# Gate and up of the feed-forward projections computed as a pair, matmul by matmul into two PSUM banks

## Chip, cores and metric

The kernel runs on one core of a Trainium2 chip. The metric is the device time of one execution in microseconds; lower is better.

## What is computed

Two transformer blocks, one after the other, on a sequence of 512 tokens with 1024 features, in float32. The first block has two layers (stick-breaking attention, dilated attention), the second one layer (a gated recurrence and a differential attention, with a modulation computed from a vector). Each of the three layers ends in a feed-forward part of inner width 2816:

```python
def _swiglu(h, w_gate, w_up, w_down):
    return (jax.nn.silu(h @ w_gate) * (h @ w_up)) @ w_down
# layers 1 and 2
h = h + _swiglu(_rmsnorm(h, norm_ffn[layer]), w_gate[layer], w_up[layer], w_down[layer])
# second block
u = rmsnorm(h, norm2_w[l]) * (1.0 + sc2) + sh2
ff = (jax.nn.silu(u @ w_ffn_gate[l]) * (u @ w_ffn_up[l])) @ w_ffn_down[l]
h = h + g2 * ff
```

The products h @ w_gate and h @ w_up, three times, are what the change touches.

## The kernel before, in words

Activations lie with features on partitions: h, xh and xl have 8 tiles of 128 x 512. Each float32 product is made of three matmuls in a faster float32 form: every operand is split into a high part (rounded) and a low part (the rest), and high x high, high x low and low x high are summed in PSUM. xh and xl are the two parts of the input.

**Units.** The weights come as units: one unit holds the 8 (in some cases 6) 128 x 128 tiles that make one output tile of 128 features. For gate and up ("gu0", "gu1", "gu2") the units alternate: gate, up, gate, up, 44 per stage, in a loop of 11 rounds of 4 (j = 0 to 3). Units have a running number over the whole kernel. A unit goes through four steps, on four queues:

- SP loads it into raw (`load_units`, L260), once the unit three before it has its low split (L253 and after).
- ACT splits off the high part: whi <- raw (`split_hi`, L281 to L290). It waits for the load, and for PE to be done with the unit three before it (`mm_done` at number - 2, L289).
- DVE subtracts: wlo <- raw - whi (`split_lo`, L301).
- PE computes the product (`product`, L303 to L318): it waits for the low split, then for each of 8 tiles issues three matmuls (L314, L315, L316) into one PSUM bank and signals `mm_done` on the last.

raw, whi and wlo have four slots each. ACT and DVE split two units ahead of the one that their loop stands at (`ahead`).

**A feed-forward projection** (`ffn_act` L607, `ffn_dve` L621, `ffn_pe` L647). Unit j writes bank j. PE waits, before unit j, until DVE has read the banks two pairs back (`f.up`, L651). After each second unit (j odd) DVE waits for `mm_done` of that unit, multiplies gate and up by rstd out of PSUM (L631, L632; in the third projection plain copies, L635 and L636), ACT applies Silu (L615), DVE multiplies (L639), ACT and DVE make the high and low parts acth and actl (L617, L641). ACT loads an activation table at some of the changes between Silu and Copy.

**What stands around it.** The stage before is a residual projection of four-unit rounds (`res_pe`, `res_act`, `res_dve`), moving tiles oh and ol, whose results become h and then xh (L373) and xl (L383). POOL sums the squares of h (L406). In the first two projections the sum over partitions is a matmul with ones (`total`, L411), placed by `ffn_pe` behind the first unit's product (`behind_first`). DVE and ACT go on from it in program order: `refine` and `root` (L424, ACT L416 and L418, DVE L427 to L432) make rstd, and only after these stand the first splits of the feed-forward loop, those of units 2 and 3. Units 0 and 1 are split in the stage before. In the third projection PE sums before the stage, and DVE and ACT then make xh and xl tile by tile (`modulate_dve` L731, L739 and `modulate_act` L745); PE follows with the first unit, waiting for each tile (`ready`).

The stage behind is the down projection ("down0" to "down2") with moving tiles acth and actl.

Of the kernel before, what the change touches and what calls it, by code (L numbers as in the profile page):

```python
# [6 lines left out]
P = 128  # L7
S = 512
D = 1024
KT = D // P  # L10
# [43 lines left out]
def wait(eng, signal, value):  # L54

    if isinstance(value, int) and value <= 0:
        return
    if isinstance(signal, Since):
        eng.wait_ge(signal.sem, value + signal.base)
    else:  # L60
        eng.wait_ge(signal, value)
# [31 lines left out]
def build(nc, a, out):  # L93
    ctx = ExitStack()
    with ctx:
# [3 lines left out]
        def place(name, shape, dtype, at=None):  # L99
            size = int(np.prod(shape[1:])) * {F32: 4, F32R: 4, BF16: 2, U8: 1}[dtype]  # L100
            size = -(-size // 32) * 32
            if at is None:
                at, top[0] = top[0], top[0] + size
            t = nc.alloc_sbuf_tensor_at(name, shape, dtype, offset=at)
            return t

        def sem(name):
            return ctx.enter_context(nc.semaphore(name))
# [6 lines left out]
        xh = place("xh", [P, KT, S], F32R)  # L115
        xl = place("xl", [P, KT, S], F32R)
        raw = place("raw", [P, 4, UNIT], F32)
        whi = place("whi", [P, 4, UNIT], F32R)
        wlo = place("wlo", [P, 4, UNIT], F32R)
# [107 lines left out]
        ps = ctx.enter_context(nc.psum_tensor("ps", [P, 8, S], F32))  # L227
# [5 lines left out]
        lo_done = sem("lo_done")  # L233
        mm_done = sem("mm_done")
        phases = []
        before, used = 0, [0] * 4
        for name, count, body, ring in (("qkv", 8, 3, 3), ("o_a", 2, 4, 4), ("gu0", 11, 4, 4), ("down0", 4, 6, 3),
# [4 lines left out]
            u = Units(a[name], count, body, ring, before, used, widths)  # L242
# [38 lines left out]
        def split_hi(act, u, pos):  # L281

            if pos is None:
                return
            t, j = pos
            s, n = u.slot(j), u.widths[j] * P
            act.wait_ge(landed[s], u.landings(t, j))

            wait(act, mm_done, u.number(t, j) - 2)  # L289
            act.activation(whi[:, s, 0:n], raw[:, s, 0:n], ACT.Copy).then_inc(hi_done, 1)  # L290

        def split_lo(eng, u, pos, in_turn=False):
# [11 lines left out]
        def product(pe, u, t, j, bank, hi, lo, k0=0, start=True, stop=True, ready=None):  # L304

            pe.wait_ge(lo_done, u.number(t, j) + 1)
            s, n = u.slot(j), u.widths[j]
            for k in range(n):
                w = slice(k * P, (k + 1) * P)
                if callable(ready):  # L310
                    ready(k0 + k)
                elif ready is not None:
                    wait(pe, ready, k0 + k + 1)
                pe.matmul(ps[:, bank], whi[:, s, w], hi[:, k0 + k], start=start and k == 0, stop=False)  # L314
                pe.matmul(ps[:, bank], whi[:, s, w], lo[:, k0 + k], start=False, stop=False)  # L315
                mm = pe.matmul(ps[:, bank], wlo[:, s, w], hi[:, k0 + k], start=False,  # L316
                               stop=stop and k == n - 1)
            mm.then_inc(mm_done, 1)  # L318

        def hold(eng, signal, value):  # L320


            wait(eng, signal, value)
            if not isinstance(value, int):
                eng.sem_inc(held[eng], 1)
# [82 lines left out]
        def total(pe, r, bank):  # L408

            wait(pe, r.added, KT + 1)  # L410
            pe.matmul(ps[:, bank], ones[:, :], sqsum[:, :], start=True, stop=True).then_inc(r.total.sem, 1)  # L411
# [123 lines left out]
        def res_act(act, u, r, gain):  # L535
            per = 1 if u.body == 4 else 3

            def body(t, end=False):
                for j in range(u.body):
                    split_hi(act, u, ahead(u, t, j, end))  # L540
                    if j % per == per - 1:
                        m = t * (u.body // per) + (j // per)
                        residual_hi(act, r, m, gain)
                        residual_sq(act, r, m, (j // per) % 2)
            body(0)
            if u.count > 2:
                with act.Fori(1, u.count - 1) as t:
                    body(t)
            body(u.count - 1, True)
            root(act, r)  # L550
# [26 lines left out]
        def res_pe(pe, u, r, hi, lo, ready, ada=None, sum_now=True):  # L577

            per = 1 if u.body == 4 else 3

            def body(t):
                for j in range(u.body):
                    m = t * (u.body // per) + (j // per)
                    if j % per == 0 and per == 1:
                        wait(pe, r.h_new, m - 3)
                    elif j % per == 0:
                        wait(pe, r.h_new, m - 1)
                    k0 = 8 * (j % per)
                    first = isinstance(t, int) and t == 0 and j < per
                    product(pe, u, t, j, j // per, hi, lo, k0, start=j % per == 0, stop=j % per == per - 1,  # L590
                            ready=ready if first else None)
                    if ada is not None:

                        if j:
                            ada_tile(pe, ada, t, j - 1)
                        elif not isinstance(t, int):
                            ada_tile(pe, ada, t - 1, 5)
            body(0)
            if u.count > 1:
                with pe.Fori(1, u.count) as t:  # L600
                    body(t)
            if ada is not None:
                ada_tile(pe, ada, u.count - 1, 5)
            if sum_now:
                total(pe, r, 7)

        def ffn_act(act, u, f):  # L607
            def body(t):
                for j in range(4):
                    split_hi(act, u, ahead(u, t, j, False))  # L610
                    if j % 2:
                        i = j // 2
                        n = 2 * t + (i + 1)
                        wait(act, f.gate, n)
                        act.activation(tmp[i][:, :], tmp[i][:, :], ACT.Silu).then_inc(f.silu.sem, 1)  # L615
                        hold(act, f.prod, n)
                        act.activation(acth[:, 2 * t + i], tmp[2 + i][:, :], ACT.Copy).then_inc(f.hi.sem, 1)  # L617
            with act.Fori(0, u.count) as t:
                body(t)
# [27 lines left out]
        def ffn_pe(pe, u, f, ready, behind_first=None):  # L647

            def body(t):
                for j in range(4):  # L650
                    wait(pe, f.up, 2 * t + (j // 2 - 1))  # L651
                    first = isinstance(t, int) and j == 0
                    product(pe, u, t, j, j, xh, xl, ready=ready if first else None)
                    if first and behind_first is not None:
                        total(pe, behind_first, 7)
            body(0)
            with pe.Fori(1, u.count) as t:
                body(t)
# [398 lines left out]
        def _(act):  # L1057
            act.wait_ge(const_in, 32)
            act.wait_ge(filled, 1)
            setup_act(act)  # L1060
            split_hi(act, U["qkv"], (0, 0))
            split_hi(act, U["qkv"], (0, 1))
            for m in range(KT):
# [456 lines left out]
        def _(pe):  # L1520
# [11 lines left out]
            def stage_g(t):  # L1532
                for j in range(3):
                    if j == 0:
                        wait(pe, qkv_out, 3 * t)
                    elif j == 1:
                        if isinstance(t, int) and t == 0:
                            wait(pe, rin.rstd, 1)
                        wait(pe, v_tok, t)
                    else:  # L1540
                        pe.wait_ge(qkv_out, 3 * t + 1)
                    first = leading(t) and j == 0
                    product(pe, u, t, j, 6 + j % 2, xh, xl, ready=rin.x_lo if first else None)
                    if first:
                        total(pe, rin, 7)
# [302 lines left out]
```

## Time and profile before

| | |
|---|---|
| three runs | 2268.95, 2269.93, 2271.29 us; median 2269.93 |
| profiled execution, span from first to last instruction | 2266.9 us |
| PE (matmul) busy | 2076.2 us, 92% |
| PEld (weight loads) busy | 1622.6 us, 72% |
| DVE, ACT, POOL busy | 1192.0, 842.0, 328.7 us |
| mean granted TensorE clock | 0.943 |
| projections gate/up: first matmul of each | 377.16, 1060.33, 1875.30 us |

No other time is recorded for the profiled execution than its span; the median of the runs is 3.0 us above it. The profile's busy time of PE overstates the work, since matmuls are pipelined and each row lasts longer than its step: the cadence has to be read from starts. PEld is the loading of weights, which runs beside the matmul before. A clock of 1.00 is 2.4 GHz, 0.50 is 1.2 GHz.

### The profile page before, as it was taken

The numbers are of one execution on the slowest core, as the hardware profiler recorded it, in microseconds if no ns is written. First come the engines' busy times: TensorE is split into PE (matmuls) and PEld (weight loads), VectorE is DVE, ScalarE is ACT, GpSimd is POOL, SyncE is SP. The second block draws the span as 40 slices with busy tenths as digits, with TensorE's granted clock in tenths as the row PEclk, the third lists the DMA queues.
The fourth block names the chain that finished last, engine by engine and source line by source line (L and its number), as shares of the span: only waits on it lengthen the run. The fifth ranks groups of instructions, "written<-read, shape, count | busy, mean of one in ns | idle before, by whom it ended". The sixth has DMA issues, their size and how long they took to land.

```text
span 2266.9 us, 25387 instructions
## 1 busy us (share of the span) xinstructions
PE 2076.2 (92%) x9000; PEld 1622.6 (72%) x9000; DVE 1192.0 (53%) x1566; ACT 842.0 (37%) x1098; POOL 328.7 (15%) x285
## 2 busy tenths in 40 slices
PE   6999989999999799989999999487759788999997
PEld 4767667888888577757888888375546566888885
DVE  4423235444488645435444488777875545444323
ACT  4443434434422233334444322343333324443321
POOL 2000001000011144431000011354421110000000
PEclk9999889999999799999999999699969799999998
DMA  3101102332355211102332355121002022223331
GB/s 118 56 32 52 37 28 84 99 104 93 90 191 193 88 56 56 56 30 86 97 102 97 96 186 200 57 72 50 28 30 73 28 75 74 93 93 104 93 93 53
DMA packets 53108, 189.38 MB, mean 84 GB/s; under 512 B 5936, under 2 KB 6448, under 8 KB 52928
## 3 DMA queue, kind: packets, MB, share of 16 engines
q1 hardware_dynamic: 45504, 160.85, 21.6%
q0 software_dynamic: 7552, 27.86, 3.7%
q8 instruction: 30, 0.49, 0.1%
q14 instruction: 22, 0.18, 0.0%
HBM read 186.59 MB, written 2.10 MB: 83 GB/s over the span
## 4 chain that ended last, share of the span: by engine, by line
PE 77%; DVE 10%; issue 6%; ACT 3%; POOL 2%; DMA 0%; SPq 0%; DVEq 0%; ACTq 0%; POOLq 0%
PE ps L314 21%; PE ps L315 21%; PE ps L316 21%; PE ps L1556 2%; PE ps L759 2%; PE ps L794 2%; PE ps L1590 1%; PE ps L1574 1%; PE ps L777 1%; DVE wlo L301 1%; PE ps L1579 1%; DVE tmps L670 1%; POOL qlev L1034 1%; POOL sqsum L406 1%; DVE amat L1439 1%
## 5 line engine op out<-in xcount | busy, mean ns | idle before, releaser
L314 PE MATMUL ps<-xh,whi 128*128 128x512 f32 x1536 | 611.3, 398 | 28.5 <-DVE xl L739 16.4
L315 PE MATMUL ps<-xl,whi 128*128 128x512 f32 x1536 | 604.9, 394 | 0.0
L316 PE MATMUL ps<-xh,wlo 128*128 128x512 f32 x1536 | 604.5, 394 | 0.0
L301 DVE TENSOR_TENSOR wlo<-raw,whi 128x1024 fp32r<-128x1024 f32 (+1 forms) x292 | 367.2, 1267 | 233.8 <-ACT whi L290 229.6
L290 ACT ACTIVATE whi<-raw 128x1024 fp32r<-128x1024 f32 (+1 forms) x304 | 313.9, 1038 | 286.4 <-PE ps L316 277.9
L314 PEld LDWEIGHTS ps<-xh,whi 128*128 128x128 f32 x1536 | 293.4, 191 | 103.5 <-issue 25.4
L316 PEld LDWEIGHTS ps<-xh,wlo 128*128 128x128 f32 x1536 | 292.6, 191 | 61.8
L315 PEld LDWEIGHTS ps<-xl,whi 128*128 128x128 f32 x1536 | 293.4, 191 | 60.3 <-issue 0.5
L314 PE MATMUL ps<-acth,whi 128*128 128x512 f32 x528 | 212.1, 402 | 0.2
L406 POOL TENSOR_TENSOR sqsum<-sqsum,tmps 128x512 f32<-128x512 f32 x64 | 86.1, 1346 | 856.8 <-ACT tmps L376 850.6
L316 PE MATMUL ps<-acth,wlo 128*128 128x512 f32 x528 | 208.6, 395 | 0.0
L315 PE MATMUL ps<-actl,whi 128*128 128x512 f32 x528 | 208.3, 395 | 0.0
L615 ACT ACTIVATE tmps<-tmps 128x512 f32<-128x512 f32 x66 | 41.7, 632 | 292.5 <-DVE tmps L631 193.0
L316 PEld LDWEIGHTS ps<-acth,wlo 128*128 128x128 f32 x528 | 99.2, 188 | 23.6
L314 PEld LDWEIGHTS ps<-acth,whi 128*128 128x128 f32 x528 | 99.4, 188 | 22.0 <-issue 0.3
L315 PEld LDWEIGHTS ps<-actl,whi 128*128 128x128 f32 x528 | 99.4, 188 | 21.7
L631 DVE TENSOR_TENSOR tmps<-ps,rstd 128x512 f32<-128x512 f32 x44 | 30.4, 692 | 133.2 <-PE ps L316 133.2
L391 POOL DMA_DIRECT2D wada<-in_ada x24 | 13.2, 552 | 573.3 <-DVE actl L641 483.4
L873 POOL TENSOR_SCALAR prob<-prob,small 128x512 f32<-128x512 f32 (+1 forms) x64 | 74.5, 1182 | 68.4 <-DVE small L855 68.4
L376 ACT ACTIVATE tmps<-h 128x512 f32<-128x512 f32 (+1 forms) x56 | 34.9, 623 | 121.2 <-DVE h L567 72.8
L641 DVE TENSOR_TENSOR actl<-tmps,acth 128x512 f32 (+1 forms) x66 | 45.7, 693 | 64.9 <-ACT acth L617 64.9
L314 PE MATMUL ps<-oh,whi 128*128 128x512 f32 x192 | 77.1, 402 | 1.1 <-DVE ol L928 1.1
(234 smaller groups left out, 2686.8 us busy)
## 6 DMA issues: line engine op xcount, KB each, us to landing
raw<-in_gu SPq DMA_DIRECT2D x132, 512.0 KB, 3.4
raw<-in_down SPq DMA_DIRECT2D x48, 512.0 KB, 3.8
raw<-in_qkv SPq DMA_DIRECT2D x24, 512.0 KB, 3.4
wada<-in_ada POOLq DMA_DIRECT2D x24, 512.0 KB, 3.6
tmps<-in_ada POOLq DMA_DIRECT2D x24, 512.0 KB, 3.8
raw<-in_qkvb SPq DMA_DIRECT2D x24, 512.0 KB, 3.3
raw<-in_down SPq DMA_DIRECT2D x24, 384.0 KB, 3.1
raw<-in_recur SPq DMA_DIRECT2D x16, 512.0 KB, 3.4
```

Source lines behind the costliest of these rows:

```text
L290: act.activation(whi[:, s, 0:n], raw[:, s, 0:n], ACT.Copy).then_inc(hi_done, 1)
L301: eng.tensor_tensor(wlo[:, s, 0:n], raw[:, s, 0:n], whi[:, s, 0:n].bitcast(F32), ALU.subtract).then_inc(lo_done, 1)
L314: pe.matmul(ps[:, bank], whi[:, s, w], hi[:, k0 + k], start=start and k == 0, stop=False)
L315: pe.matmul(ps[:, bank], whi[:, s, w], lo[:, k0 + k], start=False, stop=False)
L316: mm = pe.matmul(ps[:, bank], wlo[:, s, w], hi[:, k0 + k], start=False, stop=stop and k == n - 1)
L406: pool.tensor_tensor(sqsum[:, :], sqsum[:, :], sq[m % 2][:, :], ALU.add).then_inc(r.added.sem, 1)
L615: act.activation(tmp[i][:, :], tmp[i][:, :], ACT.Silu).then_inc(f.silu.sem, 1)
L641: dve.tensor_tensor(actl[:, 2 * t + i], tmp[2 + i][:, :], acth[:, 2 * t + i].bitcast(F32), ALU.subtract).then_inc(f.lo.sem, 1)
L759: mm = pe.matmul(tri_ps[i][:, OFF[b]:OFF[b] + w], q[rows, c * P:(c + 1) * P], k[rows, 0:w], start=True, stop=True, skip_group_check=True)
L794: mm = pe.matmul(o, v, prt[i][:, OFF[b]:OFF[b] + S - b * P], start=b == 0, stop=b == NB - 1)
L873: pool.tensor_scalar(pr[i][:, w], pr[i][:, w], share[:, 4 * i + b:4 * i + b + 1], None, ALU.mult)\
L1556: pe.matmul(tri_ps[i][:, OFF[b]:OFF[b] + n], kT[rows, b * P:(b + 1) * P], qT[rows, b * P:S], start=b != 3, stop=False, skip_group_check=True)
```

## The change

A new routine takes two units at once. For each of the 8 tiles it issues six matmuls: high weights x high input for gate, then for up; high weights x low input for both; low weights x high input for both. The two go to banks j and j + 1 in turn. It waits at its start for the low split of both units. ACT's wait ahead of a high split asks, for the gate/up units, for the unit four before instead of three before. `ffn_pe` calls the routine for j = 0 and 2; the sum of squares (`total`) stands behind the first call.

```diff
-            wait(act, mm_done, u.number(t, j) - 2)
+            wait(act, mm_done, u.number(t, j) - (3 if u.name.startswith("gu") else 2))
             act.activation(whi[:, s, 0:n], raw[:, s, 0:n], ACT.Copy).then_inc(hi_done, 1)
...
+        def product_pair(pe, u, t, j, bank, hi, lo, ready=None):
+
+            pe.wait_ge(lo_done, u.number(t, j) + 2)
+            for k in range(KT):
+                w = slice(k * P, (k + 1) * P)
+                if ready is not None:
+                    wait(pe, ready, k + 1)
+                for weight, moving, step in ((whi, hi, 0), (whi, lo, 1), (wlo, hi, 2)):
+                    for n in range(2):
+                        mm = pe.matmul(ps[:, bank + n], weight[:, u.slot(j + n), w], moving[:, k],
+                                       start=k == 0 and step == 0, stop=k == KT - 1 and step == 2)
+                        if k == KT - 1 and step == 2:
+                            mm.then_inc(mm_done, 1)
...
             def body(t):
-                for j in range(4):
+                for j in (0, 2):
                     wait(pe, f.up, 2 * t + (j // 2 - 1))
                     first = isinstance(t, int) and j == 0
-                    product(pe, u, t, j, j, xh, xl, ready=ready if first else None)
+                    product_pair(pe, u, t, j, j, xh, xl, ready=ready if first else None)
                     if first and behind_first is not None:
                         total(pe, behind_first, 7)
```

## Rows read from the trace of the kernel before

**Rows 1.** The page: busy times, and the chain's shares by engine.

```profile
PE 2076.2 (92%) x9000; PEld 1622.6 (72%) x9000; DVE 1192.0 (53%) x1566; ACT 842.0 (37%) x1098; POOL 328.7 (15%) x285
...
PE 77%; DVE 10%; issue 6%; ACT 3%; POOL 2%; DMA 0%; SPq 0%; DVEq 0%; ACTq 0%; POOLq 0%
```

**Rows 2.** The page's costliest group: busy us, mean ns, idle before it.

```profile
L314 PE MATMUL ps<-xh,whi 128*128 128x512 f32 x1536 | 611.3, 398 | 28.5 <-DVE xl L739 16.4
```

**Rows 3.** Timeline, steady part of the first projection: start us, duration us, what.

```profile
480.06 0.39 PE L314 MATMUL ps<-xh,whi 128*128 128x512 f32 x1
...
487.32 0.39 PE L316 MATMUL ps<-xh,wlo 128*128 128x512 f32 x1
...
487.54 0.39 PE L314 MATMUL ps<-xh,whi 128*128 128x512 f32 x1
...
487.74 0.69 DVE L631 TENSOR_TENSOR tmps<-ps,rstd 128x512 f32<-128x512 f32 x1 [3.12 <-PE ps L316]
...
498.42 0.39 PE L314 MATMUL ps<-xh,whi 128*128 128x512 f32 x1
```

**Rows 4.** Timeline, PE in the third down projection, the first and the seventh of seven matmuls.

```profile
2149.61 0.39 PE L314 MATMUL ps<-acth,whi 128*128 128x512 f32 x1
...
2151.01 0.39 PE L314 MATMUL ps<-acth,whi 128*128 128x512 f32 x1
```

**Rows 5.** Timeline, the splits of one pair's units in the first projection.

```profile
492.04 2.21 ACT L290 ACTIVATE whi<-raw 128x1024 fp32r<-128x1024 f32 x2
...
493.13 2.38 DVE L301 TENSOR_TENSOR wlo<-raw,whi 128x1024 fp32r<-128x1024 f32 x2 [1.56 <-ACT whi L290]
```

**Rows 6.** Timelines of DVE and PE, the start of the first projection, in order of time.

```profile
374.81 1.52 DVE L301 TENSOR_TENSOR wlo<-raw,whi 128x1024 fp32r<-128x1024 f32 x1 [0.72 <-ACT whi L290]
...
377.16 0.40 PE L314 MATMUL ps<-xh,whi 128*128 128x512 f32 x1
...
382.65 1.02 PE L411 MATMUL ps<-sqsum,ones 128*128 128x512 f32 x2
...
388.21 2.36 DVE L301 TENSOR_TENSOR wlo<-raw,whi 128x1024 fp32r<-128x1024 f32 x2 [0.30 <-ACT whi L290]
...
389.49 0.50 PE L314 MATMUL ps<-xh,whi 128*128 128x512 f32 x1 [0.33 <-DVE wlo L301]
```

**Rows 7.** The same timelines, the start of the second projection.

```profile
1065.82 1.02 PE L411 MATMUL ps<-sqsum,ones 128*128 128x512 f32 x2
...
1071.38 2.36 DVE L301 TENSOR_TENSOR wlo<-raw,whi 128x1024 fp32r<-128x1024 f32 x2 [0.30 <-ACT whi L290]
...
1072.66 0.50 PE L314 MATMUL ps<-xh,whi 128*128 128x512 f32 x1 [0.33 <-DVE wlo L301]
```

**Rows 8.** Windows: us, busy us by engine (instructions), PEclk, DMA share, GB/s.

```profile
309.30:320.00 10.70, 3.36 (x12) 1.90 (x12) 4.47 (x4) 8.48 (x8) 0.00 (x0) 0.50 0.00 0
320.00:326.40 6.40, 6.40 (x25) 6.11 (x25) 1.34 (x1) 1.02 (x1) 0.00 (x0) 0.50 0.01 3
...
1875.30:1879.50 4.20, 4.20 (x9) 2.47 (x9) 4.13 (x6) 2.07 (x3) 0.00 (x0) 0.50 0.00 0
```

**Rows 9.** Timelines of DVE and PE, the start of the third projection, in order of time.

```profile
1874.40 0.75 DVE L739 SCALAR_TENSOR_TENSOR xl<-tmps,mod,xh 128x512 fp32r<-128x512 f32 x1
...
1875.30 0.77 PE L314 MATMUL ps<-xh,whi 128*128 128x512 f32 x1 [6.71 <-DVE xl L739]
...
1875.86 0.63 PE L315 MATMUL ps<-xl,whi 128*128 128x512 f32 x1
1876.29 0.63 PE L316 MATMUL ps<-xh,wlo 128*128 128x512 f32 x1
...
1883.10 1.63 DVE L739 SCALAR_TENSOR_TENSOR xl<-tmps,mod,xh 128x512 fp32r<-128x512 f32 x2
...
1886.35 2.36 DVE L301 TENSOR_TENSOR wlo<-raw,whi 128x1024 fp32r<-128x1024 f32 x2 [1.62 <-ACT whi L290]
...
1891.04 0.39 PE L314 MATMUL ps<-xh,whi 128*128 128x512 f32 x1
```

## Prediction

> **What bounds the kernel now.** First the page's busy table and the shares of the chain: TensorE is busy for 92% of the span and makes 77% of the chain that ended last [rows 1]. The costliest group is one of three alike, L314, L315 and L316 on the tiles xh and xl, 1536 matmuls each [rows 2]; the feed-forward projections issue 3 x 11 x 4 x 8 = 1056 of each, 3168 in all. So the change lies in the largest part of the bound engine, and two things decide: the cadence of its matmuls, and the places where their stream is broken.
>
> The cadence is read from the timeline of the first projection, in its steady part [rows 3]. From the start at 480.06 us to that at 498.42 us lie 81 matmuls: 18.36 / 81 = 0.2267 us each. 512 columns at 2.4 GHz are 0.2133 us, so 0.0133 us of each is something else. If this rest were the price of writing twice in a row into one bank, it would be missing wherever the bank changes. It changes once in 24 matmuls: VectorE's read of a finished pair of banks starts at 487.74 us, released by the L316 that starts at 487.32 us; the next L314, at 487.54 us, writes another bank. That step is 0.22 us. Rounding could hide 0.01 us once, but not over the stretch: 18.36 us hold at least three changes of bank, and three times 0.0133 us saved would move the phase by 0.04 us; yet from 480.06 to 487.54 us, with one change, there are 33 steps of 0.2267, and from 487.54 to 498.42 us, with two, 48 steps of 0.2267. A change of bank saves nothing that shows.
>
> What does alter the cadence is seen in the down projection: 1.40 us for six matmuls, 0.2333 each, the same engine and shapes with another moving tile [rows 4].
>
> **The change, part by part.** PE keeps its 3168 matmuls, 48 to a pair, each with its weight load, and gets half the waits. Order and data: weights and moving tiles are the same ones, in the same slots. I cost the new order at nothing per matmul, by [rows 3]. The bounds for it are 0.2133 us (array alone) and 0.2333 us [rows 4]: 3168 x 0.0133 = 42 us less, or 3168 x 0.0067 = 21 us more. The value sits at 0.2267 because that row is of the same tiles.
>
> *The Trainium skill, "TensorE: Matmul & The Clock Gate", section "Back-to-back issue gap", gives N / 2.4 + 2.5 ns for a warm matmul, 216 ns here. The trace disagrees for the old order, with 226.7 ns; were the new order to reach the page's figure, the estimate would be 3168 x 10.7 ns = 34 us less. It is weighed as a rival below.*
>
> *Steady state, splits.* A pair now needs the split weights of both its units before its first matmul; before, the second was needed 5.44 us later. ACT may split a unit when the unit four before it is done (it was: three before), so both units of the next pair can be split while a pair runs. In the slower of the two alternating pairs (with a table load ahead) ACT does both from 492.04 to 494.25 us and DVE both until 493.13 + 2.38 = 495.51 us [rows 5]; the pair that uses them starts at 498.42 us [rows 3]. 2.9 us of cover are left, so this costs nothing. Evacuation starts where it did, after the pair's last matmul, and each bank pair is written again only a whole pair (10.9 us) later. The loader on SP waits for the low splits alone, in the same order; these come no later in the steady part, so its loads don't either.
>
> *Start of the first and second projection.* Here a cover is removed. The matmul that sums the squares (L411) stands behind the first product. Everything else waits for it in program order: DVE's refinement, ACT's root, a table load, and only then ACT's and DVE's splits of units 2 and 3. Before, unit 1 (24 matmuls, 5.44 us) ran on PE beside that chain: L411 starts at 382.65, unit 2 at 389.49 us, 6.84 us later, with 0.33 us idle [rows 6]. Now L411 follows the pair, so it starts at 382.65 + 5.44 = 388.09 us. PE then has nothing to do until both low splits are done: the two took 388.21 to 390.57 us, the first thus until some 389.39 us, and PE picked it up 0.1 us later; the second would be picked up at 390.67 us, 8.02 us after L411's start. Units 2 and 3 start at 388.09 + 8.02 = 396.11 us, where unit 2 started at 389.49: **6.6 us later**. The second projection has the same offsets (L411 at 1065.82, splits until 1073.74, unit 2 at 1072.66 us [rows 7]): 1065.82 + 5.44 + 8.02 - 1072.66 = 6.6 us again. Together 13.2 us. That the first pair also needs unit 1's low split costs nothing: it is done at 374.81 + 1.52 = 376.33 us, the stage starts at 377.16 us [rows 6].
>
> *The clock behind this stall.* PE is idle from 388.09 + 1.02 = 389.11 to 396.11 us, 7.0 us. In the stretch 309.3 to 320.0 us PE was idle for 10.70 - 3.36 = 7.34 us, and in the 6.4 us behind it the granted clock stood at 0.50, its lower level of 1.2 GHz [rows 8]; behind the gap of 6.71 us that ended at 1875.30 us it did for 4.2 us [rows 8, 9]. At this level a matmul takes 0.43 us (1875.86 to 1876.29 us [rows 9]), so of each low microsecond 1 - 0.2267 / 0.4267 = 0.47 us is lost: 2.0 to 3.0 us a stall. I take 2.5, both gaps being about as near; twice: 5.0 us. Bound from below: nothing, were the clock to stay up.
>
> *Start of the third projection.* No sum is awaited there. PE follows the low parts of the input as DVE makes them, the first at 1875.15, the last at 1884.73 us, seven steps of some 1.4 us [rows 9]; three matmuls per part leave PE idle between, six fill the time. From 1875.30 us some 9.5 matmuls at the low clock take it to 1879.5 us, the other 38.5 take 8.75 us: the pair ends at 1888.2 us, and no part is late for it (matmul 42, the last part's first, is due at 1886.9 us). Units 2 and 3 are split until 1886.35 + 2.36 = 1888.71 us, so pair 1 starts at 1888.8 us, where unit 2 started at 1891.04: **2.2 us earlier**. The bounds are 0 and 2.2.
>
> **Sum.** 13.2 + 5.0 - 2.2 = 16.0 us on the profiled span of 2266.9 us, 2282.9 us. The median of the runs, 2269.9 us, lies 3.0 us above that span, and I carry this over: 2285.9, so **2286 us**, slower by 0.7%. The forecast's own bounds: without a drop of the clock 13.2 - 2.2 = 11.0 us more than before (2281), with 3.0 us a stall and no gain in the third stage 19.2 (2289).
>
> **Rivals.**
>
> *A shorter cadence (faster).* The rest of 0.0133 us goes when consecutive matmuls write different banks, perhaps because at a single change the weight loads still hold the old phase. For it: the rest exists, and no row shows banks taken in turn over a whole stream. Against it: the unbroken phase of [rows 3]. Full size 42 us less, beside the 16.0 us above: 2269.9 - 42 + 16 = 2244 us. It decides from 16.0 / 3168 = 5 ns a matmul on; a part of it, between 4 and 6 ns, would come out as no change. Chance 0.14, 0.04 of it for such a part.
>
> *A longer cadence.* The new neighbours (wlo loaded while xh streams, whi while xl does) bring PE into the 0.2333 us of [rows 4]. For it: that cadence exists for other moving tiles. Against it: in the old order three different neighbourhoods all ran at 0.2267. It gives 2286 + 21 = 2307 us. Chance 0.07.
>
> *Late splits in the steady state.* If ACT could not take the second split at once, it would take it behind the pair's end, and PE would wait for one high and one low split, about 1.1 + 1.2 us by [rows 5]: 2.3 us at each of 63 pair changes, 145 us, some 2430 us in all. The relaxed wait at L289 speaks against it. Chance 0.02. That the change does not do what it says can hardly be: order and banks are written out in the code.
>
> *No stall where I see one,* the sum being hidden otherwise: nothing in the program order allows it; 0.02, ending within 0.2% of before.
>
> **How the numbers follow.** The forecast has 0.75. 0.2%, 4.5 us, is about what a measurement of this kernel can tell from no change. Faster: 0.14 - 0.04 = 0.10. Same: 0.04 + 0.02 = 0.06. Slower: 0.75 + 0.07 + 0.02 = 0.84. The range is the forecast's own, 2281 to 2289, widened by some 5 us on both sides for a cadence that moves by 1 to 2 ns (3 to 6 us over 3168 matmuls): 2276 to 2294 us. It leaves out the rivals' 0.25, but for their small sizes, which fall inside it: some 0.2.
>
> **What the changed profile would show.** Idle time of some 7 us ahead of the first matmul of unit 2 in the first two projections, released by the low split, and the granted clock at half behind it; L411 5.4 us later from the stage's start; in the third projection hardly any idle time between the first 48 matmuls. In the steady part, starts 0.2267 us apart and no idle time at pair changes. A mean matmul duration away from 389 ns and starts 0.213 to 0.22 us apart would make the prediction wrong on the fast side, 0.233 on the slow side; idle time ahead of every second pair would point to the splits.

## The result, and the profile after

| | before | after |
|---|---|---|
| median of 4 runs each | 2270.61 us | 2283.30 us (2281.65 to 2285.36) |
| ratio | | 1.0058, 95% interval 1.0044 to 1.0071 |
| span of the profiled execution | 2266.9 us | 2280.2 us |
| first projection, first matmul to first one of the down projection | 240.94 us | 249.53 us |
| second | 240.94 us | 249.84 us |
| third | 244.22 us | 242.10 us |

The kernel became 12.7 us slower; 2286 were forecast, in a range of 2276 to 2294. The last three rows hold the change: + 8.6, + 8.9 and - 2.1 us, together + 15.4. The span grew by 13.4 (before rounding): the other stages, whose code is the same, were 2 us shorter in this execution. That is scatter; the stretch between the second and the third projection took 574.0 us before, 568.3 after, and 568.1 to 574.1 in the profiles of the experiments on order and waits below.

The page of the kernel after: busy times, the chain's shares, and the group that replaces [rows 2] in the three projections.

```profile
PE 2073.7 (91%) x9000; PEld 1623.6 (71%) x9000; DVE 1188.8 (52%) x1566; ACT 835.1 (37%) x1098; POOL 327.4 (14%) x285
...
PE 77%; DVE 10%; issue 6%; ACT 3%; POOL 2%; DMA 1%; SPq 0%; DVEq 0%; ACTq 0%; POOLq 0%
...
L329 PE MATMUL ps<-xh,whi 128*128 128x512 f32 x1056 | 328.4, 392 | 20.8 <-DVE wlo L301 14.1
```

Averages over the kernel say nothing here: PE is as busy as before [rows 1]. The last column does. Of the 20.8 us that PE idled ahead of this group, 14.1 ended with a low split; before, a wait of this kind was 0.33 us [rows 6, 7].

The start of the first projection, timelines of PE and DVE merged in order of time (start us, duration us, what, in brackets the idle time before and what ended it). It answers to [rows 6]; L425 is L411 of before.

```profile
390.77 1.02 PE L425 MATMUL ps<-sqsum,ones 128*128 128x512 f32 x2
...
396.32 2.36 DVE L301 TENSOR_TENSOR wlo<-raw,whi 128x1024 fp32r<-128x1024 f32 x2 [0.30 <-ACT whi L290]
...
398.73 1.22 PE L329 MATMUL ps<-xh,whi 128*128 128x512 f32 x2 [6.94 <-DVE wlo L301]
```

The same of the second projection, which answers to [rows 7].

```profile
1082.95 1.02 PE L425 MATMUL ps<-sqsum,ones 128*128 128x512 f32 x2
...
1088.49 2.36 DVE L301 TENSOR_TENSOR wlo<-raw,whi 128x1024 fp32r<-128x1024 f32 x2 [0.30 <-ACT whi L290]
...
1090.90 1.22 PE L329 MATMUL ps<-xh,whi 128*128 128x512 f32 x2 [6.94 <-DVE wlo L301]
```

From the sum's start to the next pair are 7.96 us in the first and 7.95 us in the second, with 6.94 us of idle PE in both; the splits end at 398.68 and 1090.85 us, 0.05 us ahead of PE's start.

Windows of the kernel after around these stalls (us, busy us by engine, PEclk, DMA share, GB/s), to be read with [rows 8]:

```profile
391.80:396.20 4.40, 0.00 (x0) 0.00 (x0) 2.77 (x4) 3.58 (x5) 0.00 (x0) 1.00 0.00 0
396.30:403.00 6.70, 4.27 (x10) 3.40 (x11) 5.39 (x7) 4.83 (x6) 0.00 (x0) 0.50 0.49 157
403.10:413.00 9.90, 9.90 (x45) 8.16 (x44) 2.84 (x4) 0.67 (x2) 0.00 (x0) 1.00 0.36 106
1090.00:1095.90 5.90, 5.00 (x12) 3.93 (x13) 4.62 (x7) 3.79 (x5) 0.00 (x0) 0.50 0.59 181
```

The column before the last two is the granted clock. It is full while PE idles up to 396.2 us, half from 396.3 to 403.0 us, which covers the end of the gap and the first 4.3 us of the new pair, and full again. In the second projection it is half for 5.0 us of matmuls.

The start of the third projection, which answers to [rows 9]:

```profile
1890.12 1.19 PE L329 MATMUL ps<-xh,whi 128*128 128x512 f32 x2 [6.70 <-DVE xl L753]
...
1901.18 2.36 DVE L301 TENSOR_TENSOR wlo<-raw,whi 128x1024 fp32r<-128x1024 f32 x2 [1.62 <-ACT whi L290]
...
1902.80 0.61 PE L329 MATMUL ps<-xh,wlo 128*128 128x512 f32 x2
1903.60 0.72 PE L329 MATMUL ps<-xh,whi 128*128 128x512 f32 x2 [0.18 <-DVE wlo L301]
```

No idle time is left within the first 48 matmuls, and the second pair starts 13.48 us after the first, where unit 2 started 15.74 us after unit 0 (1875.30 to 1891.04 us).

The steady part of the first projection, PE, the same pair of tiles 102 matmuls apart:

```profile
500.17 0.61 PE L329 MATMUL ps<-xh,whi 128*128 128x512 f32 x2
...
523.29 0.62 PE L329 MATMUL ps<-xh,whi 128*128 128x512 f32 x2
```

23.12 / 102 = 0.2267 us, with the bank changing at every matmul: to the last digit the cadence of [rows 3]. And DVE there, the splits of a pair and the evacuation behind it:

```profile
504.40 2.36 DVE L301 TENSOR_TENSOR wlo<-raw,whi 128x1024 fp32r<-128x1024 f32 x2 [1.56 <-ACT whi L290]
510.00 0.69 DVE L645 TENSOR_TENSOR tmps<-ps,rstd 128x512 f32<-128x512 f32 x1 [3.24 <-PE ps L329]
```

Both low splits are done at 506.76 us, the pair ends at 510 us: the cover of some 3 us is there.

### The profile page after: what moved, and what is told of

Same layout as the page of the kernel before. It is cut to its first block, busy times and chain, and to the rows that moved or that the text cites. A ratio compares the mean times of both kernels' runs of the same rounds, so it can differ in the third digit from the quotient of the medians.

```text
span 2280.2 us, 25327 instructions
## 1 busy us (share of the span) xinstructions
PE 2073.7 (91%) x9000; PEld 1623.6 (71%) x9000; DVE 1188.8 (52%) x1566; ACT 835.1 (37%) x1098; POOL 327.4 (14%) x285
## 4 chain that ended last, share of the span: by engine, by line
PE 77%; DVE 10%; issue 6%; ACT 3%; POOL 2%; DMA 1%; SPq 0%; DVEq 0%; ACTq 0%; POOLq 0%
PE ps L329 31%; PE ps L314 10%; PE ps L315 10%; PE ps L316 10%; PE ps L1570 2%; PE ps L773 2%; PE ps L808 2%; PE ps L1604 1%; DVE wlo L301 1%; PE ps L1588 1%; PE ps L791 1%; DVE tmps L684 1%; PE ps L1593 1%; POOL qlev L1048 1%; POOL sqsum L420 1%
## 5 line engine op out<-in xcount | busy, mean ns | idle before, releaser
L290 ACT ACTIVATE whi<-raw 128x1024 fp32r<-128x1024 f32 (+1 forms) x304 | 307.1, 1034 | 243.1 <-PE ps L316 235.8
L329 PE MATMUL ps<-xh,whi 128*128 128x512 f32 x1056 | 328.4, 392 | 20.8 <-DVE wlo L301 14.1
L329 PE MATMUL ps<-xl,whi 128*128 128x512 f32 x1056 | 327.6, 392 | 0.0
L329 PE MATMUL ps<-xh,wlo 128*128 128x512 f32 x1056 | 326.9, 391 | 0.0
L329 PEld LDWEIGHTS ps<-xl,whi 128*128 128x128 f32 x1056 | 199.9, 189 | 41.9
L314 PE MATMUL ps<-xh,whi 128*128 128x512 f32 x480 | 198.5, 414 | 19.6 <-DVE xl L753 8.8
L315 PE MATMUL ps<-xl,whi 128*128 128x512 f32 x480 | 194.7, 406 | 0.0
L316 PE MATMUL ps<-xh,wlo 128*128 128x512 f32 x480 | 193.9, 404 | 0.0
L316 PEld LDWEIGHTS ps<-xh,wlo 128*128 128x128 f32 x480 | 94.8, 198 | 20.8
```

Of the source, the lines that this page charges most:

```text
L329: mm = pe.matmul(ps[:, bank + n], weight[:, u.slot(j + n), w], moving[:, k], start=k == 0 and step == 0, stop=k == KT - 1 and step == 2)
```

## The experiments

Each was compared with runs of the kernel before on the same chip, taken with it; their median was 2269.81 us for experiments 1, 2, 3 and 6, 2270.29 us for 4, 5, 7 and 8, and 2267.85 us (one run) for 9 and 10.

**1. The sum moved into the first pair.** The rest is as in the change.

```diff
             for k in range(KT):
                 w = slice(k * P, (k + 1) * P)
+                if inside is not None and k == 4:
+                    total(pe, inside, 7)
...
-                    if first and behind_first is not None:
-                        total(pe, behind_first, 7)
```

> The sum of squares (the matmul with ones) is moved from behind the first pair into it, behind its fourth tile, so that 24 matmuls stand ahead of it and 24 behind it, as before the change; the order of the others stays that of the change. Theory (the loss is the lost cover of the chain sum, root, splits): pair 1 starts 5.49 + 8.02 = 13.5 us after the stage's start in the first two projections (unit 2 did 12.3 us after it before the change), with some 1.5 us idle ahead of it, released by the low split, and no low clock behind it; the third projection keeps its gain of 2.1 us. Time: before + 2 x 1.2 - 2.1, about the time of before, 2270 to 2272 us. Rival (the order of the matmuls or the pairs' waits cost the time in the steady part): it stays at 2283 us.

Measured: 2270.40 us, ratio to before 1.0005 (0.9991 to 1.0018). The stages took 242.07, 242.04 and 242.08 us. PE in the first one:

```profile
386.73 1.02 PE L427 MATMUL ps<-sqsum,ones 128*128 128x512 f32 x2
...
394.70 0.73 PE L331 MATMUL ps<-xh,whi 128*128 128x512 f32 x2 [1.47 <-DVE wlo L301]
```

Again 7.97 us from the sum to the next pair, but 24 matmuls of it are covered: 1.47 us idle. Moving one matmul, with order, banks and waits as in the change, took back the whole loss. The rival, a cost in the steady part, is out.

**2. The order inside a pair alone undone.** Waits, relaxed split wait and place of the sum as in the change; gate's 24 matmuls first, then up's.

```diff
-            for k in range(KT):
+            for n in range(2):
+                for k in range(KT):
...
-                for weight, moving, step in ((whi, hi, 0), (whi, lo, 1), (wlo, hi, 2)):
-                    for n in range(2):
+                    for weight, moving, step in ((whi, hi, 0), (whi, lo, 1), (wlo, hi, 2)):
```

> The change with its waits, its relaxed split wait and the sum behind the pair, but inside a pair all 24 matmuls of gate come ahead of those of up, so the bank changes once in 24. Theory (bank order costs and gives nothing): the cadence stays 226.67 ns in the steady part, the two stalls of some 7 us stay, the third projection loses its gain of 2.1 us, since three matmuls per arriving tile leave idle time: about 2285 us, 2 us above the change. Rival (taking banks in turn shortens or lengthens the cadence and something else hid it): 3168 matmuls times that difference, over 6 us from the change for 2 ns.

Measured: 2286.20 us, ratio 1.0077 (1.0053 to 1.0101); stages 249.86, 249.82 and 244.24 us. PE at the starts of the first and the third stage:

```profile
391.05 1.02 PE L425 MATMUL ps<-sqsum,ones 128*128 128x512 f32 x2
399.01 0.80 PE L329 MATMUL ps<-xh,whi 128*128 128x512 f32 x1 [6.94 <-DVE wlo L301]
...
1896.68 0.50 PE L329 MATMUL ps<-xh,whi 128*128 128x512 f32 x1 [0.30 <-DVE xl L753]
```

The stalls stand as they were without any alternation of banks, the cadence is 0.2267 us, and the third stage is back at the 244.22 us of before, with PE idle ahead of tiles again. So the alternation is worth 2.1 us at one place, by giving PE twice the work per arriving tile, and nothing per matmul. The medians of the two kernels differ by 2.9 us, with intervals that overlap; the stage lengths carry this, not the medians.

**3. The splits ahead of the chain.** With the sum inside the pair, the splits of units 2 and 3 are put ahead of ACT's root and DVE's refinement. They are then left out of the first round of the feed-forward loop; to do so, the edit also writes out the first round of ACT's loop ahead of it (not among the lines shown).

```diff
             body(u.count - 1, True)
+            if u.name in ("o_a", "o_b"):
+                gu = U["gu0" if u.name == "o_a" else "gu1"]
+                split_hi(act, gu, (0, 2))
+                split_hi(act, gu, (0, 3))
             root(act, r)
...
+                split_lo(dve, gu, (0, 2))
+                split_lo(dve, gu, (0, 3))
             refine(dve, r, 7)
```

> As the kernel with the sum inside the first pair, and besides the high and low splits of units 2 and 3 stand ahead of ACT's root and DVE's refinement instead of behind them. Theory: nothing of the chain is left in PE's way in the first two projections; pair 1 starts 48 matmuls and 0.46 us for the sum after the stage's start, 11.4 us, 0.9 us earlier than unit 2 before the change, and the third projection keeps its 2.1 us: 2270.6 - 1.8 - 2.1, about 2267 us, a little faster than both kernels. Rival (the root would come late and the evacuation of pair 0 with it, so that the next pair's splits are late): idle time ahead of pair 2, no gain over the kernel with the sum inside the pair alone.

Measured: 2267.54 us, ratio 0.9989 (0.9978 to 1.0); stages 240.31, 240.31 and 241.38 us. PE never idles in the first two. The low splits end at 383.58 + 2.66 = 386.24 us, 0.38 us behind the sum's start and ahead of DVE's first work on the sum:

```profile
383.58 2.66 DVE L301 TENSOR_TENSOR wlo<-raw,whi 128x1024 fp32r<-128x1024 f32 x2 [0.72 <-ACT whi L290]
...
385.86 1.02 PE L427 MATMUL ps<-sqsum,ones 128*128 128x512 f32 x2
...
386.92 0.69 DVE L440 TENSOR_SCALAR var<-ps 128x512 f32<-128x512 f32 x1 [0.68 <-PE ps L427]
```

**4. The splits ahead of the chain, the sum left behind the pair.** These are the additions of experiment 3 to ACT and DVE, made to the kernel after the change.

> The change with the sum left behind the first pair, and the splits of units 2 and 3 put ahead of ACT's root and DVE's refinement. Theory (only the splits in the chain's wake keep PE waiting, not the place of the sum): pair 1 follows the sum at once in the first two projections, no gap of 7 us and no low clock. The chain then ends 5.3 us after the sum's start, the evacuation of pair 0 with the next two splits takes another 6.3 us, 11.6 us in all beside 11.3 us of matmuls: at most 0.5 us idle ahead of pair 2. Time 2267 to 2269 us. Rival (the place of the sum costs by itself): idle time of several us ahead of pair 1 or 2, 2273 us or more.

Measured: 2267.80 us, ratio 0.999 (0.998 to 1.0001); stages 240.31, 240.31 and 241.57 us. PE, and DVE's splits for the pair after next:

```profile
390.90 1.02 PE L425 MATMUL ps<-sqsum,ones 128*128 128x512 f32 x2
391.36 1.03 PE L329 MATMUL ps<-xh,whi 128*128 128x512 f32 x2
...
399.99 2.36 DVE L301 TENSOR_TENSOR wlo<-raw,whi 128x1024 fp32r<-128x1024 f32 x2 [0.26 <-ACT whi L290]
```

The sum stands where the change put it and costs PE its 0.46 us only. So its place did no harm by itself: the harm was that the next pair's splits stood behind everything that waits for it. The late evacuation just fits: the splits end at 402.35 us, and no idle time follows. (It fits in a version whose ACT loads fewer tables, see below experiment 5; whether it would with them was not tried.)

**5. The unit-by-unit kernel with the splits ahead.** The same additions to the kernel before. The early high split of unit 3 has to ask for the unit four before instead of three before, so this wait is relaxed with it.

> The kernel before the change, unit by unit, with only the splits of units 2 and 3 put ahead of ACT's root and DVE's refinement in the first two projections. Theory: the 0.33 us of idle PE ahead of unit 2 and the 0.1 us of restart go, some 0.6 us a stage, 1.2 us in all: 2268.6 us. So of the 2.3 us by which the pairs with splits first beat the kernel before, 1.2 come from the splits and some 2 us less than that from the pairs in the third projection; it lies 1 to 2 us above the pairs with splits first.

Measured: 2270.88 us, ratio 1.0005 (0.9994 to 1.0015); stages 240.31, 240.31 and 244.22 us. The profile has the expected 0.63 us less in each of the first two stages; the runs cannot tell 1.3 us from nothing. Beside experiment 3 it shows where a difference between pairs and units lies: in the third stage alone.

**What experiments 3 to 5 changed besides.** With the first round of its loop written out, ACT loads a table 16 times in the whole kernel instead of 79, and this goes for experiments 7 to 10 too. On the page of experiment 3 ACT has 63 instructions fewer and is busy for 750 us instead of 835:

```profile
PE 2072.0 (91%) x9000; PEld 1622.8 (72%) x9000; DVE 1189.9 (53%) x1566; ACT 750.4 (33%) x1035; POOL 327.5 (14%) x285
```

In the stall of the change one such load stands between the sum and the high splits:

```profile
393.86 1.28 ACT L290 ACT_TABLE_LOAD   x1
```

So it could account for 1.3 of the 6.94 us at most; the rest went with the order of the splits. In the steady part PE waited for no split with the loads either. In the third stage the load that stood ahead of the first high splits is gone, and DVE's splits follow the input's last low part after 0.20 us instead of 1.62 us:

```profile
1884.78 2.36 DVE L301 TENSOR_TENSOR wlo<-raw,whi 128x1024 fp32r<-128x1024 f32 x2 [0.20 <-ACT whi L290]
```

Pair 1 starts there 12.89 us (experiment 3) and 13.08 us (experiment 4) after the stage's start without any wait, instead of 13.48 us. That is most of the 0.7 and 0.5 us by which these third stages are shorter than that of the change.

**6. The old wait ahead of a high split, with pairs.**

```diff
-            wait(act, mm_done, u.number(t, j) - (3 if u.name.startswith("gu") else 2))
+            wait(act, mm_done, u.number(t, j) - 2)
```

> The change with ACT's wait put back to the unit three before. Theory (both units of the next pair must be split while a pair runs): the second unit's splits fall behind each pair's end, 2.0 to 2.3 us of idle PE at each of 63 pair changes, 126 to 145 us: 2410 to 2430 us. Rival (cover of 2.9 us is enough either way): within 5 us of the change.

Measured: 2459.66 us in one run, span 2457.8 us; stages 305.34, 305.73 and 299.84 us. PE at two pair changes, and the sum of these waits:

```profile
482.89 0.73 PE L329 MATMUL ps<-xh,whi 128*128 128x512 f32 x2 [2.18 <-DVE wlo L301]
...
496.25 0.74 PE L329 MATMUL ps<-xh,whi 128*128 128x512 f32 x2 [2.18 <-DVE wlo L301]
```

```profile
PE ps L329 <- DVE wlo L301: 146.8, 63, 6.9
```

The mechanism is the expected one, 2.18 us of idle PE at a change. Its price was set too low: a pair now takes 13.36 us from start to start and not 10.88, so 2.48 us are lost at each change. The last matmul ahead of the idle time takes its 0.39 us in full where a step is 0.23 us, and the first two behind it take 0.12 us longer together (0.73 instead of 0.61 us). 61 such changes make 151 us. Of the 178 us between the spans 169 lie in the three stages, so 18 are left there. They fit the clock: four times in each stage the granted clock fell to 0.50 for 3.4 us, each time at one of these gaps; here the first and the ninth time (columns as above).

```profile
454.70:458.00 3.30, 3.30 (x8) 2.62 (x9) 2.15 (x4) 1.82 (x3) 0.00 (x0) 0.50 0.48 159
...
2052.10:2055.40 3.30, 3.14 (x7) 2.48 (x8) 2.13 (x5) 1.71 (x4) 0.00 (x0) 0.50 0.49 159
```

As an estimate, 12 x 3.4 us at 0.47 us lost in each are 19 us. The other 8 us lie in stages whose code is the same, in this one execution.

**7 to 10. Where the two cadences come from.** The prediction had seen 0.2267 us with xh and xl as moving tiles and 0.2333 with acth, without a reason. By the placement code each partition holds xh from byte 32896, whi from 82048, wlo from 98432 and the region of oh, acth and yh from 138496: xh lies 0 bytes modulo 256 from the weights, the others 128. Experiments 7 and 8 start from experiment 3 and move one small tile of 384 bytes, 7 to ahead of raw as shown, 8 in the same way to ahead of h:

```diff
+        small = place("small", [P, 96], F32)
         raw = place("raw", [P, 4, UNIT], F32)
...
-        small = place("small", [P, 96], F32)
```

> The kernel with the splits first and the sum inside the pair, and one small tile of 384 bytes per partition is placed ahead of raw, whi and wlo instead of behind them: these three move up by 384 bytes, xh and xl and the activations oh, acth, yh stay. Before, xh and whi start at the same remainder modulo 1024 bytes (128) and run at 226.7 ns; oh, acth and yh start at another (256) and run at 232 to 233.3. Theory A (the cadence hangs on how moving tile and weights lie to each other modulo 256 bytes): now oh, acth and yh agree with the weights modulo 256 and run at 226.7, xh and xl do not and run at 233: 4608 matmuls 6 ns dearer, 2544 cheaper, some 13 us slower than without the move. Theory B (it hangs on the moving tile's own place alone): nothing changes, 2267 us, both cadences stay where they were.

> The same with the small tile ahead of h: h, xh, xl, raw, whi and wlo all move up by 384 bytes and start at remainder 0 modulo 256, as oh, acth and yh do. Theory A: every product runs at 226.7 ns, 2544 matmuls 6 ns cheaper: 2267 - 15 = 2252 us. Theory C (the moving tile's own remainder modulo 256 decides, 128 good, 0 bad): xh and xl fall to 233 as well, 4608 x 6.2 ns = 29 us slower, 2296 us. Theory B2 (its place in the upper part of the memory decides): nothing changes.

Measured: experiment 7 2285.60 us, ratio 1.0068 (1.0042 to 1.0093); experiment 8 2257.32 us, ratio 0.994 (0.9917 to 0.9963). Groups by form in two stretches of 110 and 70 us, 450 to 560 us (first projection) and 2160 to 2230 us (third down projection); count, busy us, mean ns. Experiment 3:

```profile
L331 PE MATMUL ps<-xl,whi 128*128 128x512 f32 x163 | 50.3, 389 | 0.0
...
L314 PE MATMUL ps<-acth,whi 128*128 128x512 f32 x101 | 39.9, 395 | 0.0
```

Experiment 7:

```profile
L331 PE MATMUL ps<-xl,whi 128*128 128x512 f32 x158 | 49.7, 395 | 0.0
...
L314 PE MATMUL ps<-acth,whi 128*128 128x512 f32 x103 | 40.1, 389 | 0.0
```

Experiment 8:

```profile
L331 PE MATMUL ps<-xl,whi 128*128 128x512 f32 x163 | 50.3, 389 | 0.0
...
L314 PE MATMUL ps<-acth,whi 128*128 128x512 f32 x104 | 40.5, 389 | 0.0
```

Moving the weights alone swapped the two cadences, 389 against 395 ns and 163 against 158 matmuls in the same stretch. xh had not moved in experiment 7, so its own place does not decide; acth had not moved either and became fast. What decides is how the two lie to each other. (Theories B, B2 and C, by which a tile's own place decides, are out; experiment 8, with all of them at one remainder, is fast throughout.) The size was missed in experiment 7: 13 us more than experiment 3 were expected, 18 were measured. Experiments 9 and 10 add pads to experiment 8, one ahead of raw, one behind wlo: 64 and 32 bytes in 9, as shown, 32 and 96 in 10.

```diff
+        place("pad1", [P, 16], F32)
         raw = place("raw", [P, 4, UNIT], F32)
...
+        place("pad2", [P, 8], F32)
         vec = place("vec", [P, NVEC], F32)
```

> From the kernel with all tiles moved (every moving tile starts at the same remainder modulo 256 bytes as the weights, 226.7 ns everywhere): a pad of 64 bytes ahead of raw and one of 32 bytes behind wlo. Now xh and xl lie at the weights' remainder + 192, oh, acth and yh at the weights' remainder + 32. If only an exact match modulo 256 is fast, both groups run at 232 to 233.3 ns and the time is some 44 us above the kernel with all moved, 2300 us. If the 232 to 233.3 belongs to an odd multiple of 128 alone (where every slow case so far lay), both run at 226.7 and the time stays at 2257. A third value below 226.7 for some distance would be new.

> The same with pads of 32 and 96 bytes: xh and xl at the weights' remainder + 224, oh, acth and yh at + 96. The same alternatives: 2300 us if only an exact match is fast, 2257 if only a distance of 128 is slow; with the kernel of pads 64 and 32 it gives four distances more between the two known ones.

Measured, one run each: 2292.66 and 2301.94 us. The three feed-forward projections took the same time in both, 247.25, 247.25 and 248.5 us; 8 of the 9 us between the two runs lie ahead of the first one, which starts at 378.43 and 386.54 us. The same groups of experiment 9:

```profile
L333 PE MATMUL ps<-xl,whi 128*128 128x512 f32 x158 | 49.7, 396 | 0.0
...
L316 PE MATMUL ps<-acth,whi 128*128 128x512 f32 x100 | 39.5, 395 | 0.0
```

In experiment 10 they are:

```profile
L333 PE MATMUL ps<-xl,whi 128*128 128x512 f32 x157 | 49.4, 396 | 0.0
...
L316 PE MATMUL ps<-acth,whi 128*128 128x512 f32 x101 | 39.8, 394 | 0.0
```

| start of moving tile minus start of weights, modulo 256 bytes | mean step at the full clock |
|---|---|
| 0 | 226.8 to 227.7 ns |
| 32, 96, 192, 224 | 233.2 to 233.5 ns |
| 128 | 232.4 to 233.0 ns |

Each value is the mean step of a kernel's unbroken streams with one pair of moving tiles (such as xh and xl), stretches at the lower clock left out. All six distances tried fit one rule: equal modulo 256 bytes is fast, the five others are slow. A distance of 768 modulo 1024 is among the fast ones (oh, acth and yh in experiments 7 and 8), so equality modulo 1024 is not needed.

Experiment 8 brought 10 us where 15 were expected. From first to last matmul, against experiment 3, the third down projection took 119.45 us instead of 122.96, 6.7 ns less for each of 527 steps; the second took 125.38 instead of 127.81 us; the first 128.57 instead of 128.73 us, though its tiles lie the same way. The three streams of oh together became 2.6 us shorter. In the first two down projections DVE works beside PE on the modulation vector and is busy for 88% and 86% of the time (experiment 3):

```profile
620.70:749.00 128.30, 128.02 (x571) 103.58 (x570) 112.76 (x87) 33.45 (x41) 23.62 (x32) 1.00 0.55 184
1303.70:1431.00 127.30, 127.26 (x571) 103.61 (x570) 109.30 (x82) 29.96 (x34) 22.58 (x32) 1.00 0.55 187
```

So this work may hold the first one at its length; PE waits for DVE there three times in experiment 8, 0.8 us in all, and never in experiment 3. It did not keep the second from gaining 2.4 us, and it was not tried. In experiment 7 the same three took 128.71, 125.50 and 119.50 us, so it gained as little where it was to gain, which accounts for most of its 5 us too much.

## Why the prediction was right

**The cadence.** "I cost the new order at nothing per matmul, by [rows 3]": measured 0.2267 us before and after. A stream whose phase did not move at single bank changes did not move when every matmul changed bank; experiment 2 shows the same from the other side. The figure of 216 ns in the Trainium skill, "TensorE: Matmul & The Clock Gate", section "Back-to-back issue gap", is not reached in either order. The rival of a shorter cadence, at 0.14, fell, and so did that of a longer one: 0.2333 us has to do with the place of the tiles and not with order.

**The stall.** 6.6 us a stage were forecast, with 8.02 us from the sum to the next pair and 7.0 us of idle PE. Measured: 7.95 us and 6.94 us. The difference is PE's start, 0.05 us behind the second low split where 0.1 us was taken. By program order, the earlier timeline and one shift of 5.44 us the whole chain came out to within 0.1 us, and experiments 1 and 4 show that it is this chain.

**The clock.** 4.2 to 6.4 us at half clock were taken over from two gaps of the same length. Measured: 4.3 and 5.0 us. The stages' growth beyond the stall is 8.59 - 6.55 = 2.0 and 8.90 - 6.55 = 2.35 us; 2.5 each were taken. That this size came out right is luck in part. At both gaps from which it was taken the clock had fallen before the gap began, while PE was still at work, as these windows of the kernel before show; in the change it was still full for the first 4.4 us of one gap and 5.1 us of the other. No run here explains why the stretches behind came out alike.

```profile
309.40:312.60 3.20, 3.20 (x11) 1.83 (x10) 1.45 (x1) 1.69 (x2) 0.00 (x0) 0.50 0.00 0
...
1865.90:1868.50 2.60, 1.99 (x2) 0.50 (x2) 0.00 (x0) 0.00 (x0) 0.56 (x1) 0.50 0.00 0
```

With the shorter stalls of experiment 1 (1.47 us) nothing of it is left: its stages are 242.07 us, the 1.1 us more than before that the stall alone explains.

**The third stage.** 2.2 us earlier were forecast, 2.1 us measured, and experiment 2 puts them down to the order.

**The sum.** By stages 16.0 us were forecast and 15.4 measured. The medians give 12.7, with an interval of 10 to 16 us. The forecast of 2285.9 us lies 2.6 us above the measured median. 0.6 of them are in its terms. The other 2.0 are the stages whose code is the same, which were that much shorter in the profiled execution, as above. The carried offset held: the median stood 3.0 us above the profiled span before and 3.1 us after. The median before is itself 0.7 us higher with a fourth run (2270.61 for 2269.93 us), so that the difference of the medians is 12.7 us.

**Late splits.** The relaxed wait and 2.9 us of cover were read rightly; what the rival would have cost was given as 145 us, and experiment 6 measured 178 from span to span, 169 of them in the three stages. The term that was too small is the price of a broken stream, 2.3 us a change where 2.48 were lost; the lower clock behind some of the gaps was not in it.

## What to carry to other kernels

When work is merged into larger pieces, look at what stood between the pieces: here one small matmul started a chain on two other engines, DVE and ACT, and the second piece was its cover. Put what the next piece needs (the splits) ahead of such a chain on each in-order queue; then the merge itself is free. Whether consecutive matmuls share a bank made no difference to these streams of 512 columns; whether moving tile and weights start at the same byte modulo 256 made 3% of a matmul's step, and costs only the order of allocation.

## What the runs showed that was not expected

The alignment rule above: 226.7 ns against some 233 ns a matmul, for a placement that nobody had chosen. With one tile of 384 bytes moved to the front, the pairs and the early splits, the kernel takes 2257.32 us, 0.6% less than before the change and the fastest version here; 10 of these 13 us came with the tile.

A gap of 1.47 us left the stage's length without any loss by the clock, and two of 6.94 us drew 4.3 and 5.0 us of the lower level behind them. With 2.18 us of idle time at every change, as in experiment 6, it stood at the lower level twelve times for 3.4 us, so here gaps that are short each did cost clock as they came again and again.

Writing out one round of ACT's loop removed 63 of 79 table loads, 85 us of ACT's busy time. ACT was not what PE waited for, and beyond these 0.5 to 0.7 us in the third stage no run shows a gain by it.
